# Meta and parameter waits behind the compressed norm, second attention reordered, reciprocal first in covered norms

## What is computed

```python
def mla_mixer(x, ...):
    h = x @ w_in                       # 1024 -> 512 + 256 + 64
    c_q, c_kv, k_r = split(h)
    c_q = rms_norm(c_q, q_norm)        # the compressed norm
    c_kv = rms_norm(c_kv, kv_norm)
    q = c_q @ w_uq; k = c_kv @ w_uk; v = c_kv @ w_uv
    ...

def forgetting_attention(h, w_q, w_o, k, v, c):
    s = q k^T * scale + c_q - c_k      # causal mask
    return (softmax(s) @ v) @ w_o

def layer_norm(x, g, b):
    mu = mean(x); var = mean(square(x - mu))
    return (x - mu) * rsqrt(var + eps) * g + b
```

## Time and profile before

| | |
|---|---|
| median of 3 runs | 1794.31 us |
| profiled execution, its own time | 1793.77 us |
| its span, first to last instruction | 1791.9 us |
| mean granted clock of TensorE | 0.999 of full speed |
| ACT, DVE, POOL busy | 969.8, 1134.4, 117.9 us |
| DMA | 297.74 MB, 166 GB/s on average |

### The profile page before, as it was taken

How to read it: one execution, slowest core, us unless ns; L and a number is a source line. 1 busy time by engine, 2 the same in 40 slices (tenths; PEclk the granted TensorE clock), 3 DMA queues, 4 the chain that set the end, 5 groups by cost and what they waited for, 6 DMA issues and landing times.

```text
span 1791.9 us, 32993 instructions
## 1 busy us (share of the span) xinstructions
PE 1770.7 (99%) x14168; PEld 1735.1 (97%) x14168; DVE 1134.4 (63%) x1835; ACT 969.8 (54%) x1531; POOL 117.9 (7%) x124
## 2 busy tenths in 40 slices
PE   8999999999999999999999999999999999999998
PEld 8999999997899999999999999999999999899998
DVE  6776888565479885755546665554655556765554
ACT  5665766466367664744435454443554444764443
POOL 1001000110020001100011020001100002020002
PEclk9999999999999999999999999999999999999999
DMA  6424455544345555455444445555444554245552
GB/s 213 144 95 153 170 182 185 187 166 158 125 142 193 186 186 186 155 185 176 177 176 153 173 143 182 176 176 177 153 170 165 188 184 158 95 162 182 186 188 95
DMA packets 85056, 297.74 MB, mean 166 GB/s; under 512 B 10512, under 2 KB 13456, under 8 KB 84912
## 3 DMA queue, kind: packets, MB, share of 16 engines
q1 hardware_dynamic: 84176, 294.85, 47.2%
q10 hardware_dynamic: 736, 0.80, 0.1%
HBM read 294.57 MB, written 1.05 MB: 165 GB/s over the span
## 4 chain that ended last, share of the span: by engine, by line
PE 92%; DVE 3%; ACT 2%; DMA 1%; issue 1%; SPq 0%; POOL 0%; ACTq 0%; DVEq 0%; POOLq 0%
PE ps L1433 27%; PE ps L1431 27%; PE ps L1432 27%; PE ps L1462 2%; PE ps L1467 2%; PE ps L1463 2%; PE ps L1484 1%; DVE w_lo L888 1%; PE ps L1442 1%; DMA par<-params 1%; PE ps L1699 1%; PE ps L1701 1%; ACT x L462 1%; ACT w_hi L424 0%; PE ps L1898 0%
## 5 line engine op out<-in xcount | busy, mean ns | idle before, releaser
L888 DVE TENSOR_TENSOR w_lo<-raw,w_hi 128x1024 fp32r<-128x1024 f32 x557 | 689.6, 1246 | 348.7 <-ACT w_hi L424 226.6
L424 ACT ACTIVATE w_hi<-raw 128x1024 fp32r<-128x1024 f32 x557 | 580.6, 1051 | 178.1 <-DMA raw<-stream 155.5
L1431 PE MATMUL ps<-a_hi,w_hi 128*128 128x256 f32 (+1 forms) x2088 | 595.5, 285 | 5.7 <-DVE w_lo L888 5.5
L1433 PE MATMUL ps<-a_hi,w_lo 128*128 128x256 f32 (+1 forms) x2088 | 592.9, 284 | 0.0
L1432 PE MATMUL ps<-a_lo,w_hi 128*128 128x256 f32 (+1 forms) x2088 | 592.4, 284 | 0.0
L1431 PEld LDWEIGHTS ps<-a_hi,w_hi 128*128 128x128 f32 x2088 | 394.9, 189 | 7.9 <-DVE w_lo L888 7.1
L1433 PEld LDWEIGHTS ps<-a_hi,w_lo 128*128 128x128 f32 x2088 | 395.3, 189 | 0.0
L1432 PEld LDWEIGHTS ps<-a_lo,w_hi 128*128 128x128 f32 x2088 | 393.3, 188 | 0.5
L1431 PE MATMUL ps<-h_hi,w_hi 128*128 128x256 f32 (+1 forms) x1336 | 379.4, 284 | 0.3 <-DVE w_lo L888 0.3
L1433 PE MATMUL ps<-h_hi,w_lo 128*128 128x256 f32 (+1 forms) x1336 | 378.0, 283 | 0.0
L1432 PE MATMUL ps<-h_lo,w_hi 128*128 128x256 f32 (+1 forms) x1336 | 377.4, 282 | 0.0
(11 more groups left out here) (266 smaller groups left out, 1855.8 us busy)
## 6 DMA issues: line engine op xcount, KB each, us to landing
raw<-stream SPq DMA_DIRECT2D x557, 512.0 KB, 3.3
x<-xT SPq DMA_DIRECT2D x2, 512.0 KB, 5.0
out<-x SPq DMA_DIRECT2D x8, 128.0 KB, 1.7
work<-pT ACTq DMA_DIRECT2D x2, 256.0 KB, 2.6
par<-params SPq DMA_DIRECT2D x1, 283.5 KB, 11.2
tmp<-causal ACTq DMA_DIRECT2D x1, 208.0 KB, 2.4
con<-consts SPq DMA_DIRECT2D x1, 194.5 KB, 9.5
tmp<-pos SPq DMA_DIRECT2D x1, 128.0 KB, 9.5
```

Source lines behind the costliest of these rows:

```text
L424: nc.scalar.activation(w_hi[:, u % SLOTS, :], raw[:, u % SLOTS, :], ACT.Copy).then_inc(w_hi_ready, 1)
L888: nc.vector.tensor_tensor(w_lo[:, u % SLOTS, :], raw[:, u % SLOTS, :], w_hi[:, u % SLOTS, :].bitcast(F32), ALU.subtract).then_inc(w_lo_rea ...
L1431: nc.tensor.matmul(dst, wh, xh, start=first, stop=False, skip_group_check=True)
L1433: return nc.tensor.matmul(dst, wl, xh, start=False, stop=last, skip_group_check=True)
```

## The change

ACT waits for the meta tokens and the parameters, and rounds the meta tokens, only behind the compressed norm; DVE's low part of the meta tokens moves behind the key units. In the covered norms DVE takes the reciprocal before it waits for the spread mean. In the second attention, from iteration 3 on, the mix of tile i - 1 stands ahead of the turn of tile i on PE, and its high part ahead of the copies on ACT; the rounding of `att_o` units moves to the end of the iteration (what was the query's last `hi_next` to the start of iteration 2) and their subtraction one iteration later; behind the loop the squares stand ahead of the rounding and the residuals ahead of the subtraction, one subtraction goes behind the norm, and the norm pools seven tiles.

```diff
--- before.py
+++ after.py
@@ -371,7 +371,7 @@
         aq_copied = sem("aq_copied")
 
         cols_of = {name: slice(0, T) if name in ("ffn2", "conv", "ffn3") else TOK for name in LN}
-        pooled_of = {name: 6 if name in ("gla", "att") else 7 for name in LN}
+        pooled_of = {name: 6 if name == "gla" else 7 for name in LN}
 
         def each_unit(phase, body, n=None, first=0):
             n = n or dict(PHASES)[phase]
@@ -580,9 +580,6 @@
                 nc.scalar.activation(a_hi[:, n, TOK], x[:, n, TOK], ACT.Copy).then_inc(x_hi_ready, 1)
             for u in range(1, AHEAD):
                 hi(u)
-            act.wait_ge(in_meta, 16)
-            nc.scalar.activation(b_hi[:, :, 0:META], x[:, :, 0:META], ACT.Copy).then_inc(meta_split, 1)
-            act.wait_ge(in_par, 16)
 
             u = BASE["mla_in"]
             for n in range(7):
@@ -628,6 +625,9 @@
                     nc.scalar.activation(vm[:, m, 512 * i:512 * i + 512], ps[:, banks[m], :], ACT.Copy).then_inc(v_copied, 1)
 
             warm(ACT.Exp)
+            act.wait_ge(in_meta, 16)
+            nc.scalar.activation(b_hi[:, :, 0:META], x[:, :, 0:META], ACT.Copy).then_inc(meta_split, 1)
+            act.wait_ge(in_par, 16)
             for i in range(2):
                 u = BASE["mla_qr"] + i
                 mla_q_rope(u, i, u % BANKS)
@@ -815,36 +815,47 @@
                 u = BASE["att_q"] + n
                 act.wait_ge(unit_done, u + 1)
                 nc.scalar.activation(a_q[:, n, :], ps[:, ATT_Q_BANK[n], 0:SEQ], ACT.Copy, scale=ATT_SCALE).then_inc(aq_copied, 1)
-                hi_next(u)
+                if n < 7:
+                    hi_next(u)
+
+            def att_mixed(t):
+                a = 16 + t
+                act.wait_ge(mixed, a + 1)
+                nc.scalar.activation(h_hi[:, t, TOK], ps[:, 2 + a % 2, 0:SEQ], ACT.Copy).then_inc(h_hi_ready, 1)
 
             for n in range(3):
                 query(n)
             for i in range(-2, 9):
                 a = 16 + i
+                if i == 2:
+                    hi_next(BASE["att_q"] + 7)
                 if i + 2 < 8:
                     exponentials(a + 2, 144, 272, sm_a)
                 if i + 5 < 8:
                     query(i + 5)
-                if 3 <= i < 6:
-                    hi_next(BASE["att_o"] + i - 3)
+                if 3 <= i:
+                    att_mixed(i - 1)
                 if 0 <= i < 8:
                     act.wait_ge(turned, a + 1)
                     if i >= 2:
                         act.wait_ge(mixed, a - 1)
                     nc.scalar.activation(pt_a[:, a % 2, :], ps[:, 6 + a % 2, 0:384], ACT.Copy).then_inc(turned_sb, 1)
                     nc.scalar.activation(ptm_a[:, a % 2, :], ps[:, 2 + a % 2, SEQ:512], ACT.Copy).then_inc(turned_sb, 1)
-                if 1 <= i:
-                    act.wait_ge(mixed, a)
-                    nc.scalar.activation(h_hi[:, i - 1, TOK], ps[:, 2 + (a - 1) % 2, 0:SEQ], ACT.Copy).then_inc(h_hi_ready, 1)
+                if 1 <= i < 3:
+                    att_mixed(i - 1)
+                if 3 <= i < 6:
+                    hi_next(BASE["att_o"] + i - 3)
             warm(ACT.Sqrt)
-            squares(LN["att"], range(4), TOK)
-            for i in range(3, 8):
-                if i < 7:
-                    hi_next(BASE["att_o"] + i)
-                if i == 6:
-                    hi_next(BASE["att_o"] + 7)
-                if i >= 4:
-                    squares(LN["att"], [i], TOK)
+            squares(LN["att"], range(5), TOK)
+            u = BASE["att_o"]
+            hi_next(u + 3)
+            squares(LN["att"], [5], TOK)
+            hi_next(u + 4)
+            hi_next(u + 5)
+            squares(LN["att"], [6], TOK)
+            hi_next(u + 6)
+            squares(LN["att"], [7], TOK)
+            hi_next(u + 7)
             layer_norm(LN["att"], TOK)
             ffn(5)
             layer_norm(LN["ffn5"], TOK)
@@ -904,7 +915,7 @@
                 nc.vector.scalar_tensor_tensor(y[:, n, cw], x[:, n, cw], ALPHA, ps[:, bank, 0:cw.stop - cw.start],
                                                ALU.mult, ALU.add).then_inc(y_ready, 1)
 
-            def layer_norm(k, cw, split):
+            def layer_norm(k, cw, split, covered=False):
                 n_cols = cw.stop - cw.start
                 blocks, rows = len(token_blocks(cw)), token_blocks(cw)[0][1]
                 mean, spread = row_mean[0:rows, 0:blocks], row_var[0:rows, 0:blocks]
@@ -924,11 +935,15 @@
                     nc.vector.tensor_tensor(y[:, n, cw], y[:, n, cw], ps[:, 7, 0:n_cols], ALU.subtract).then_inc(dve_step, 1)
                     return steps[0]
 
-                dve.wait_ge(mean_spread, k + 1)
-                lessened = [less_mean(0)]
+                lessened = []
+                if not covered:
+                    dve.wait_ge(mean_spread, k + 1)
+                    lessened.append(less_mean(0))
                 dve.wait_ge(std_ready, k + 1)
                 nc.vector.reciprocal(spread, spread).then_inc(rstd_ready, 1)
-                lessened += [less_mean(1), less_mean(2)]
+                dve.wait_ge(mean_spread, k + 1)
+                for n in range(len(lessened), 3):
+                    lessened.append(less_mean(n))
                 dve.wait_ge(rstd_spread, k + 1)
 
                 def scaled(n):
@@ -1157,11 +1172,6 @@
             lo_next(u + 2)
             dve.wait_ge(rope_tab, 2)
             link(nc.vector.tensor_scalar(sinT, sinT, ccol("rope_sign"), None, ALU.mult))
-            dve.wait_ge(meta_split, 1)
-            nc.vector.tensor_tensor(b_lo[:, :, 0:META], x[:, :, 0:META], b_hi[:, :, 0:META].bitcast(F32),
-                                    ALU.subtract).then_inc(meta_lo, 1)
-
-
             for n in range(3, 6):
                 lo_next(u + n)
             dve.wait_ge(c_sums, 1)
@@ -1210,6 +1220,9 @@
                 lo_next(BASE["mla_qn"] + i)
             for i in range(2):
                 lo_next(BASE["mla_kn"] + i)
+            dve.wait_ge(meta_split, 1)
+            nc.vector.tensor_tensor(b_lo[:, :, 0:META], x[:, :, 0:META], b_hi[:, :, 0:META].bitcast(F32),
+                                    ALU.subtract).then_inc(meta_lo, 1)
             lo_next(BASE["mla_v"])
             masked(0, 0, 128, 256, sm_m, mask_m, True)
             masked(1, 0, 128, 256, sm_m, mask_m, True)
@@ -1244,7 +1257,7 @@
                     lo_next(u + i)
             layer_norm(LN["mla"], TOK, "ln0")
             ffn(0)
-            layer_norm(LN["ffn0"], TOK, "ln1")
+            layer_norm(LN["ffn0"], TOK, "ln1", True)
             embedding(0)
 
 
@@ -1345,7 +1358,7 @@
             plain("gla_o", LN["gla"], TOK)
             layer_norm(LN["gla"], TOK, "ln2")
             ffn(1)
-            layer_norm(LN["ffn1"], TOK, "ln3")
+            layer_norm(LN["ffn1"], TOK, "ln3", True)
             embedding(1)
 
 
@@ -1403,8 +1416,8 @@
                     normalized(16 + i + 1, 144, 272, sm_a)
                 for n in {-2: (1, 2), -1: (3,), 0: (4,), 1: (5,), 2: (6, 7)}.get(i, ()):
                     lo_next(BASE["att_q"] + n)
-                if 3 <= i < 6:
-                    lo_next(BASE["att_o"] + i - 3)
+                if 4 <= i < 7:
+                    lo_next(BASE["att_o"] + i - 4)
                 if 1 <= i:
                     mixed_low(16 + i - 1, H_SPLIT["att"] + i, i - 1, 2 + (16 + i - 1) % 2)
             u = BASE["att_o"]
@@ -1412,15 +1425,12 @@
                 dve.wait_ge(unit_done, u + 2 * (i // 2) + 2)
                 nc.vector.scalar_tensor_tensor(y[:, i, TOK], x[:, i, TOK], ALPHA, ps[:, i // 2, (i % 2) * SEQ:(i % 2 + 1) * SEQ],
                                                ALU.mult, ALU.add).then_inc(y_ready, 1)
-            lo_next(u + 3)
             for i in range(4, 8):
-                if i == 7:
-                    lo_next(u + i)
                 dve.wait_ge(unit_done, u + i + 1)
                 residual(LN["att"], i, ATT_O_BANK[i], TOK)
-                if i < 7:
-                    lo_next(u + i)
+                lo_next(u + i - 1)
             layer_norm(LN["att"], TOK, "ln8")
+            lo_next(u + 7)
             ffn(5)
             layer_norm(LN["ffn5"], TOK, None)
 
@@ -2064,9 +2074,11 @@
                     att_query(i + 5)
                 elif i >= 3:
                     att_out(i - 3)
+                if 3 <= i:
+                    att_mix(i - 1)
                 if 0 <= i < 8:
                     att_turn(i)
-                if 1 <= i:
+                if 1 <= i < 3:
                     att_mix(i - 1)
             att_out(6)
             att_out(7)
@@ -2076,7 +2088,7 @@
                 for k in range(KD):
                     ins = three(ps[:, ATT_O_BANK[n], 0:SEQ], *tile(u_o + n, k), h_hi[:, k, TOK], h_lo[:, k, TOK], k == 0, k == KD - 1)
                 ins.then_inc(unit_done, 1)
-            stats(LN["att"], TOK, 6)
+            stats(LN["att"], TOK, 7)
             ffn(5, a_hi, a_lo, "ln8")
             stats(LN["ffn5"], TOK, 7)
```

## The result

The changed kernel takes 1785.74 us in the median of 5 runs (1784.59 to 1785.97), the kernel before 1794.73 (1794.29 to 1796.04, 5 runs) on the same chip: ratio 0.9945, 95% interval 0.9934 to 0.9956, so 9.0 us less. The forecast was 1784.9. The profiled execution of the changed kernel took 1784.64 us, span 1782.4, against 1793.77 and 1791.9: 9.5 us of span.

A forecast was written before the change was run, and what follows sets the result against it. PE, busy 1770.7 of 1791.9 us, was taken as the bound, leaving its waits: -6.5 - 0.15 - 3.4 + 0.3 + 0.3 = -9.45 from 1793.77 gives 1784.3, plus 0.54 for the median: 1784.9 us, range 1783.2 to 1788.0.

The forecast's parts named there:

- (b): Norm after second attention: POOL's seventh tile meets subtractions, mean at 3.3 instead of 3.06; +0.3 together with (a).
- Start, -6.5: First projection: without the meta and parameter waits, PE reaches the compressed norm's sums 6.6 us earlier, counted as -6.5.
- The clock term: First projection: PE's long rest before unit 5 dropped the clock, losing 1.6 us, included in the start's gain.
- I take 0.1 off: Start: allowance of 0.1 us off 6.6 for ACT's evictions and rounding and DVE's unit 9 subtraction being late next.
- Rival B: Start: DVE's rope chain holds unit 5, gain 5.0 to 5.5 in place of 6.5; 1786.2 us; 12%.
- Moved pieces, nothing: Query and key units: the moved rounding and subtraction fall into ACT's and DVE's waits for PE, costing nothing.
- Covered norms, -0.15: Two covered norms: PE's rest before the second spread moves to the gate product; the reciprocal's slot saves 0.08 twice.
- Attention loop, -3.4: Second attention: PE's three rests go, 3.05 us, plus 0.35 or so for matmul tails beside them; bounds 0 and -3.5.
- Rivals D and E: Second attention: ring stays as slow, 1788.3 us, 6%; or mix needing the previous turn's copies slows it, 1803.3 us, 2%.
- (a): Norm after second attention: last residual no longer stands behind two `w_lo`, which would give 0.74 us.
- Rival C: Norm after second attention: POOL becomes the bound, +2.0 in place of +0.3; 1786.6 us; 12%.
- (c): After that norm: up unit 3's subtraction now stands behind the norm, so PE waits and drains; +0.3, bounds 0 and +1.2.

The follow-up runs named there:

- half-way kernels: Two runs on the kernel before: only the mix ahead of the turn, 1795.02 us; only the `att_o` rounding and subtraction moved later, 1791.96 us.
- covered norms alone: Kernel before with only the reciprocal taken ahead of the wait for the spread mean in the two covered norms: 1795.49 us, ratio 1.0001.
- mix order alone: Kernel before with only the mix ahead of the turn and its high part ahead of the copies, from iteration 3 on: 1795.02 us, ratio 0.9997.
- the kernel with the attention alone: Kernel before with only the second attention's changes, loop and the norm after it: 1791.51 us, ratio 0.9979.
- the kernel with the rest filled: Kernel before with eight dummy products put into PE's rest between units 4 and 5 of the first projection: 1794.6 us, ratio 0.9996.

## Why the prediction came out

**Total.** 9.5 off the span against 9.45 in the sum; the median 0.8 above the forecast and inside its own range of 1783.3 to 1786. That is partly luck: the start and the covered norms gave 0.5 less than forecast and ffn4 took 0.4, while the attention stage gave 1.0 more. The errors of 1.0 each way cancel; the mechanism of the start and of the loop held, that of the norm's part (b) did not.

- **Start, -6.5.** The working forward held in each step: ACT waits 1.69 for the stream (1 to 2), unit 5's subtraction at 22.37 (22.5), unit 5 on PE at 23.65 (23.75), sums at 29.39 (29.4), clock at 1.00. The clock term, 1.6 by counting matmuls, measured 1.5. The mis-sized step is "I take 0.1 off" for what is late next: 0.5 went there, 0.3 to POOL's add beside the subtractions and 0.2 to DVE's third one. Net 6.12. Rival B is out: no rest over 0.4 and sums at 29.4. The one rest was 0.39 and not 0.15.
- **Moved pieces, nothing.** Held: the offset is 6.12 at the first query product and 6.15 at 181 us, with no marked rest of PE between.
- **Covered norms, -0.15.** Measured nothing: the offset gained 0.11 over the first and lost 0.08 over the second. Its mechanism held, the rest moved to `a_hi` as written; of the 0.08 for the reciprocal's slot 0.06 did reach PE at the gate (offset 6.50 ahead of it and 6.56 at its first product in the first norm), and was gone again 15 us later.
- **Attention loop, -3.4.** Measured -3.8. All three rests went. The step that was short is the tail beside each rest: I counted 0.35 for three, where my own 0.28 less 0.12 makes 0.48, and it is 0.73 in total (23.51 - 19.73 less the 3.05 of rests), as PE also lost time at turns where no rest was marked: at tile 4's the last product starts at 1555.38 and the turn at 1555.61, 0.23 later where the spacing is 0.12. So the gain lies outside my bounds of 0 and -3.5. I had ascribed the gain to the late splits by the chain, and the half-way kernels bear that out. What I did not see is that the mix order, which I walked through step by step, is not needed. Rivals D and E are out by the periods, 3.75 and 3.05, where they needed 4.95 and 4.9 or more.
- **Its norm, (a) and (b) +0.3.** The sign was wrong: -0.45 (2.97 to 2.52). The step that failed is "both its adds now meet a subtraction: 2 x 1.6". Only the first add did (1.32); the second had started 0.04 before the subtraction and took 0.73, and it was the subtraction that grew, to 1.77, where nobody waited for it. POOL is so done 1.1 behind the last product, not 2.1, and PE comes to the sum of squares only at 1578.95; what it waited for was the first add. The mean came 2.09 after the first sums matmul, below the 2.4 that the prediction named as the sign against (b). Rival C is out. The Trainium skill ("GPSIMD Engine Reference", section "Key points") says that POOL and a DVE instruction with two SBUF inputs contend; the traces agree, 1.77 and 1.32 beside 1.23 and 0.74. What I took from it, that a seventh pooled tile is the wrong way round, did not follow: the last contention was lost by the engine with slack.
- **(c) up unit 3, +0.3.** 0.43 (offset 9.94 to 9.51), in an idle time too short for the lists to mark and the tail beside it; the price of the other place is 0.68.
- **Not in the sum:** 0.4 lost at the norm after ffn4, by a transfer that landed 4.4 after its issue and not 3.3.

In the sum: -6.12 + 0 - 3.8 - 0.45 + 0.43 + 0.4 = -9.5.

## What to carry to other kernels

When an engine in a ring of dependences also does work that nobody needs for 15 us, move that work to where the engine waits anyway; the order of the work inside the ring may then not matter. Of every wait for a transfer, ask what is queued behind it: here two waits for late arrivals, one (the meta tokens) taken away by the change and one (the norm after ffn4) left in it, held up work that had nothing to do with the data. A release of an engine ahead of its real bound (the reciprocal) moves a rest and does not shorten it; and where two engines contend, price the loss at the one that has no slack.

## What the hardware showed beyond that

**Which of DVE and POOL pays.** In the pairs of rows read, the instruction that started second was the one held up: POOL's add took 1.32 to 1.73 behind a subtraction under way (alone 0.74), the subtraction 1.77 behind an add under way (alone 1.23). The whole profile of before bears it out: its 43 adds that began inside a `w_lo` subtraction took 1.11 to 1.76, all 77 others 0.72 to 0.80; its 34 subtractions that began inside an add took 1.32 to 1.85, all 523 others 1.21 to 1.23.

**PE's clock.** It fell to its lower level (1.2 GHz, a granted 0.50) after a rest of 3.06 us in the profile of before, and with the rest cut to 0.39, or filled but for 1.30, it did not. The length of one rest does not settle it: a rest of 2.88 that ended at 23.50 saw no fall (covered norms alone), another of 2.88 that ended at 28.47 a fall at 28.00 (mix order alone). Behind a rest of 2.48 before the sums of the norm after ffn4 it fell too (window of the kernel with the mix order alone, just behind that rest), and once it fell at about 412 us in the kernel with the attention alone, behind rests of no more than 0.56, where in before the same stretch kept full clock:

```profile
1516.00:1518.00 2.00, 2.00 (x13) 2.00 (x12) 0.00 (x0) 0.00 (x0) 0.05 (x1) 0.55 0.66 248
```

```profile
412.00:414.00 2.00, 2.00 (x6) 1.54 (x5) 1.83 (x3) 2.00 (x3) 0.00 (x0) 0.50 0.66 244
```

That fall cost 1.5 us (the offset goes from 0.98 to -0.58 between 407 and 505 us), and the kernel with the rest filled had it too. The traces show three differences between executions: such a fall (1.5); the landing at ffn4 (up to 3.5 with the fall behind it); and, where ACT's wait is still at the start, the landing of the meta tokens. They were rounded at 19.89 in the kernel with the norms alone and at 18.91 in before, and the sums came 0.7 later. That these are all of the 1 to 4 us by which executions of one kernel differ is not shown, as each kernel left one trace. A gain of that size is to be read from rows, not from medians.
